# A two-mixer decoder step: a rebuilt opening, and the gate work of the first mixer moved between engines

## The reference

```python
h = _rmsnorm(x, norm_mix[i])
proj = h @ w_in                                   # (544, 4096): q, fz, i, g for 8 heads of 128
q = jax.nn.silu(q)
log_f = jnp.logaddexp(jnp.log(jnp.maximum(lb, LB_FLOOR)), jnp.log1p(-lb) + jax.nn.log_sigmoid(fz))
k = (1.0 - lb) * jax.nn.sigmoid(-fz)
o, S = _hgrn_recurrence(q, k, i, log_f, S0)       # S_t = diag(f_t) S_{t-1} + k_t v_t^T, o_t = S_t^T q_t
o = _rmsnorm(o, out_norm) * jax.nn.silu(g)
return o @ w_out, S
```

## Time and profile before

| | us |
|---|---|
| three runs, median (lowest, highest) | 1976.42 (1971.94, 1976.88) |
| the profiled execution's own time | 1976.46 |
| its span, first to last instruction | 1974.7 |
| PE busy in the span | 1811.3 |
| DVE busy | 1134.3 |
| ACT busy | 661.5 |

### The profile page before, as it was taken

One profiled execution on the slowest core, in us unless ns is written; L12 is line 12 of the kernel. 1 busy time (PEld: TensorE's weight loads), 2 busy tenths in 40 slices (PEclk: granted clock), 3 DMA queues, 4 the chain that ended last, 5 costly groups with the idle time before them and its releaser, 6 DMA issues. The chain is left out here.

```text
span 1974.7 us, 33936 instructions
## 1 busy us (share of the span) xinstructions
PE 1811.3 (92%) x13227; PEld 1714.2 (87%) x13227; DVE 1134.3 (57%) x2027; ACT 661.5 (33%) x1108; POOL 0.4 (0%) x5
## 2 busy tenths in 40 slices
PE   3899899998999999997799999999988999999997
PEld 3888888887999989997688888888867999999996
DVE  5777878785534334354666677667732643434344
ACT  1434444432212222222444455445522221222222
POOL 0000000000000000000000000000000000000000
PEclk9988989898999999998799999999957999999997
DMA  5122222222333323222112211211110333322321
GB/s 174 46 64 65 67 63 66 64 66 67 86 94 88 86 76 86 77 77 54 45 44 57 58 37 50 56 56 33 56 34 22 88 89 90 90 86 85 88 82 45
DMA packets 257436, 136.00 MB, mean 69 GB/s; under 512 B 6698, under 2 KB 255876, under 8 KB 257348
## 3 DMA queue, kind: packets, MB, share of 16 engines
q1 hardware_dynamic: 219700, 114.03, 20.4%
q10 hardware_dynamic: 37648, 20.68, 3.5%
HBM read 122.70 MB, written 12.00 MB: 68 GB/s over the span
## 5 line engine op out<-in xcount | busy, mean ns | idle before, releaser
L425 PE MATMUL pj<-xh,w_hi 128*128 128x272 f32 x2064 | 467.2, 309 | 29.8 <-DVE w_lo L1304 15.0
L425 PE MATMUL pj<-xl,w_hi 128*128 128x272 f32 x2064 | 440.4, 296 | 0.0
L425 PE MATMUL pj<-xh,w_lo 128*128 128x272 f32 x2064 | 439.4, 295 | 0.0
L865 ACT ACTIVATE w_hi<-w_raw 128x1024 fp32r<-128x1024 f32 x209 | 220.8, 1056 | 642.3 <-PE pj L425 623.9
L425 PEld LDWEIGHTS pj<-xh,w_hi 128*128 128x128 f32 x2064 | 335.6, 196 | 54.3 <-issue 26.8
L425 PEld LDWEIGHTS pj<-xl,w_hi 128*128 128x128 f32 x2064 | 338.5, 197 | 0.0
L425 PEld LDWEIGHTS pj<-xh,w_lo 128*128 128x128 f32 x2064 | 336.8, 197 | 0.0
L1304 DVE TENSOR_TENSOR w_lo<-w_raw,w_hi 128x1024 fp32r<-128x1024 f32 x209 | 254.8, 1219 | 45.9 <-ACT w_hi L865 45.7
L425 PE MATMUL pj<-oh,w_hi 128*128 128x272 f32 x1280 | 269.0, 292 | 12.7 <-DVE ol L1347 5.4
L425 PE MATMUL pj<-oh,w_lo 128*128 128x272 f32 x1280 | 266.0, 289 | 0.0
L425 PE MATMUL pj<-ol,w_hi 128*128 128x272 f32 x1280 | 266.0, 289 | 0.0
(11 more groups left out here) (275 smaller groups left out, 2050.8 us busy)
## 6 DMA issues: line engine op xcount, KB each, us to landing
w_raw<-in_mlp_w_up_dram SPq DMA_DIRECT2D x64, 512.0 KB, 3.9
w_raw<-in_mlp_w_down_dram SPq DMA_DIRECT2D x64, 512.0 KB, 3.7
w_raw<-in_hgrn_w_in_dram SPq DMA_DIRECT2D x32, 512.0 KB, 4.0
w_raw<-in_gdn_w_in_dram SPq DMA_DIRECT2D x32, 512.0 KB, 4.1
out_dram<-S ACTq DMA_DIRECT2D x16, 512.0 KB, 3.5
S<-in_state_hgrn_dram ACTq DMA_DIRECT2D x8, 512.0 KB, 4.0
w_raw<-in_hgrn_w_out_dram SPq DMA_DIRECT2D x8, 512.0 KB, 3.6
S<-in_state_gdn_dram ACTq DMA_DIRECT2D x8, 512.0 KB, 4.0
```

Of the source, the lines that this page charges most:

```text
L425: last = mm(pj[:, s, b, 0:HALF], w[:, s, k, :], v[:, k, b * HALF:(b + 1) * HALF], start=(k == 0 and a == 0), stop=(k == KT - 1 and a == 2))
L865: f(w_hi[:, c % SPLIT], w_raw[:, slot], ACT.Copy).then_inc(w_high, 1)
```

## The change

Five edits, in the program's order.

1. SP loads the identity, then all four blocks of `x` and the sample rows into five buffers without a wait, then the first four weight blocks, then the rest of `cf`, the masks (now bytes, no cast) and the two small arrays. The seven vector arrays are issued by ACT.
2. The turned blocks use PSUM banks 2, 3 and 0, 1 in turn; DVE copies blocks 0 and 2, ACT blocks 1 and 3. DVE's fills wait for nothing. The lower bounds come behind the eighth norm tile, with one more operation (`lb7`).
3. In the first norm ACT makes `xh` (a copy with a scale) and the square, DVE `xl` and the sum.
4. In a head's gate work the absolute values of fz, q, g and of the log-gate difference become ACT `Abs` instructions with the sign in the scale of the following `Exp`; K comes from ACT as one `Exp` with a bias; the factor of the log gate is folded into `Ln`, and `cd`, `cmax` and the add before the scan become one DVE operation.
5. In the tail of a head the scan, Q, level 1's differences, their exponential and its products (`d1`, `e1`, `kl1`) for the *next* head come ahead of `on`; eb and ebd come ahead of `rn`. At the head's start DVE does `d2`, `adiag`, kd, qe in that order.

```diff
@@ sync: the opening
-            sp.dma_start(cf[:], const_f).then_inc(c_in, c)
-            for stage_, part in zip(cstage, (const_u[:, 0:CU_HALF], const_u[:, CU_HALF:2 * CU_HALF])):
-                sp.dma_start(stage_, part).then_inc(c_in, c)
...
+            sp.dma_start(cf[:, 0:P], const_f[:, 0:P]).then_inc(eye_in, 16)
             for n in range(NC):
-                if n >= 2:
-                    sp.wait_ge(xs.sem, n - 1)
-                sp.dma_start(xrow[n % 2], x_prompt[0, n * P:(n + 1) * P, :]).then_inc(x_in[n % 2], 16)
+                sp.dma_start(xrow[n], x_prompt[0, n * P:(n + 1) * P, :]).then_inc(x_in[n], 16)
...
@@ scalar: the first norm
+                for i in (1, 3):
+                    sem_of(t, "t", i)
+                    s.did(f(xT[:, :, i * P:(i + 1) * P], rr[:, 0:2, :].rearrange("p a (k n) -> p (a k) n", n=P), ACT.Copy), "copy")
+                sem_of(s, "copy", 1)
+                high(0, 0)
...
+                for k in range(KT):
+                    s.did(f(xh[:, k], xT[:, k], ACT.Copy, scale=vec[:, V_MIX + k:V_MIX + k + 1]), f"hi{k}")
+                    if k >= 2:
+                        sem_of(v, f"acc{k - 2}", 0)
+                    s.did(f(sq[:, k % 2], xT[:, k], ACT.Square), f"sq{k}")
+                    if k == 1:
+                        high(0, 1)
+                lower_bounds()
@@ scalar: the gates
+                s.did(f(ng[:, row, 0:T], pr[:, row, 0:T], ACT.Abs), names[0])
+                s.did(f(ng[:, row, 0:T], ng[:, row, 0:T], ACT.Exp, scale=-1.0), names[1])
+                s.did(f(ng[:, row, 0:T], ng[:, row, 0:T], ACT.Ln, bias=1.0), names[2])
...
-                    sem_of(v, "nabs", h)
-                    s.did(f(pr[:, 1, 0:T], pr[:, 1, 0:T], ACT.Exp), "kexp")
-                    s.did(f(T1, T1, ACT.Exp), "cexp")
+                    sem_of(v, "fls", h)
+                    s.did(f(T1, ng[:, 1, 0:T], ACT.Abs, scale=-1.0, bias=hc[:, 3:4]), "nabs")
+                    s.did(f(T1, T1, ACT.Exp, scale=-1.0), "cexp")
+                    s.did(f(T1, T1, ACT.Ln, bias=hc[:, 0:1], scale=hc[:, 0:1]), "cln")
+                if slot == "K":
+                    sem_of(v, "fb", h)
+                    s.did(f(hg["K"], pr[:, 1, 0:T], ACT.Exp, bias=hc[:, 2:3]), "K")
@@ scalar: the tail of a head
+                    sem_of(v, "kl64", h)
+                    hgrn_prepare("K", nxt)
                     hgrn_prepare(7, nxt)
+                    hgrn_prepare("e1", nxt)
...
+                    hgrn_prepare(9, nxt)
                 sem_of(s, "ln", h)
                 s.did(f(sqr, sqr, ACT.Exp, scale=-0.5), "rn")
-                    hgrn_prepare(9, nxt)
@@ vector: the gates
-                    v.did(ts(T1, ng[:, 1, 0:T], hc[:, 2:3], hc[:, 1:2], ALU.add, ALU.subtract), "cd")
-                    v.did(stt(out=T1, in0=T1, scalar=-1.0, in1=T1, op0=ALU.mult, op1=ALU.min), "nabs")
-                    v.did(ts(ng[:, 1, 0:T], ng[:, 1, 0:T], hc[:, 2:3], hc[:, 1:2], ALU.add, ALU.max), "cmax")
-                    v.did(tt(ng[:, 1, 0:T], ng[:, 1, 0:T], T1, ALU.add), "lf")
+                    v.did(stt(out=ng[:, 1, 0:T], in0=ng[:, 1, 0:T], scalar=hc[:, 3:4], in1=T1, op0=ALU.max, op1=ALU.add), "lf")
+                if slot == "scan":
+                    v.did(nc.vector.tensor_tensor_scan(hg["b"], reset, ng[:, 1, 0:T], 0.0, ALU.mult, ALU.add), "scan")
+                    v.did(tt(hg["Q"], pr[:, 0, 0:T], ng[:, 0, 0:T], ALU.mult), "Q")
+                    v.did(apart_levels(0, 1), "d1")
+                    v.did(less_than_last(hg["bd"], hg["b"]), "bd")
                 if slot == 7:
                     v.did(log_sigmoid(2, T), "gls")
+                    after(s, "e1", h)
+                    v.did(scaled(0, 1), "kl1")
                     low(h * 4, U_HIN + 4)
-                if slot == 8:
...
@@ vector: a head's start
-                v.did(tt(qe, Q, eb, ALU.mult), "qe")
-                v.did(tt(kd, K, hg["bd"], ALU.mult), "kd")
-                differences(0, 1)
+                after(va, "kl1", h)
+                differences(1, 2)
                 after(t, "diag", h)
...
+                v.did(tt(kd, K, hg["bd"], ALU.mult), "kd")
+                v.did(tt(qe, Q, eb, ALU.mult), "qe")
                 low(h * 4, U_HIN + 5)
@@ vector: the tail of a head
                 if nxt is not None:
+                    hgrn_prepare("scan", nxt)
                     hgrn_prepare(7, nxt)
-                    hgrn_prepare(8, nxt)
                 out_tail(h, v, s, V_HON, hg["oo"], hg["sq"], hg["gate"], va)
```

More of the change, by code:

```diff
@@ L213, in build @@
         c_in = sem("constants_loaded")
-        x_in = [sem(f"x_loaded{n}") for n in range(2)]
+        eye_in = sem("identity_loaded")
+        vec_in = sem("vector_rows_loaded")
+        x_in = [sem(f"x_loaded{n}") for n in range(NC + 1)]
         st_in = sem("state_loaded")
@@ L225, in build @@
         VS = dict(
-            init=["masks", "fill", "vec", "cw", "lb1", "lb2", "lb3", "lb4", "lb5", "lb6"],
+            init=["fill", "vec", "cw", "lb1", "lb2", "lb3", "lb4", "lb5", "lb6", "lb7"],
             x=["copy"], xs=["copy"],
+            first=[f"{n}{k}" for k in range(KT) for n in ("lo", "acc")],
             norm=[f"{n}{k}" for k in range(KT) for n in ("acc", "hi", "lo")], normf=[f"acc{k}" for k in range(KT)],
-            ha=["cols", "fneg", "fls", "fb", "cd", "nabs", "cmax", "qneg", "qls", "lf", "gneg", "gls", "Q", "K", "scan",
-                "bd", "gate"],
-            hr=["qe", "kd", "d1", "adiag", "d2", "kl1", "d4", "kl2", "pred1", "d8", "kl4", "pred2", "d16", "kl8", "pred4",
+            ha=["cols", "fls", "fb", "qls", "lf", "scan", "Q", "d1", "bd", "gls", "kl1", "gate"],
+            hr=["d2", "adiag", "kd", "qe", "d4", "kl2", "pred1", "d8", "kl4", "pred2", "d16", "kl8", "pred4",
                 "d32", "kl16", "pred8", "S0", "S1", "S2", "S3", "d64", "kl32", "pred16", "vbig", "sdec", "kl64", "pred32",
@@ L262, in build @@
             init=["vec"], x=["t"], xs=["t"],
-            norm=["sum"], normf=["sum"],
+            first=["sum"], norm=["sum"], normf=["sum"],
             hr=["diag", "lv1", "lv2", "vT", "kdT", "lv4", "smp", "lv8", "dS", "lv16", "os", "lv32", "dSs", "lv64", "o", "ss"],
@@ L512, in level @@
                     more(tiles)
-                    pe.wait_ge(v.sem, v.after(f"kl{m}", h))
+                    if n == 0:
+                        pe.wait_ge(va.sem, va.after("kl1", h))
+                    else:
+                        pe.wait_ge(v.sem, v.after(f"kl{m}", h))
                     if n >= 2:
@@ L522, in level @@
                     t.did(last, f"lv{m}")
[L524 removed]
+                pe.wait_ge(va.sem, va.after("Q", h))
                 pe.wait_ge(st["ha"][1].sem, st["ha"][1].after("ebd", h))
@@ L1204, in _ @@
             load_state(state_hgrn, 0)
-            high(0, 0)
-            high(0, 1)
-            norm("n0", None)
-            for slot in range(3, 10):
+            first_norm()
+            for slot in (3, 4, 5, 6, "K", 7, "e1", 8, 9):
                 hgrn_prepare(slot, 0)
@@ L1807, in _ @@
             for k in range(KT):
-                norm_tile("n0", V_MIX, k)
+                first_norm_tile(k)
                 if k == 1:
                     low(0, 1)
+            lower_bounds()
+            dve.wait_ge(c_in, 16 * N_CONST)
             after(st["n0"][1], "rstd", 0)
-            for slot in range(2, 10):
+            for slot in (2, 3, 4, 5, 6, "scan", 7, 9):
                 hgrn_prepare(slot, 0)
```

254 lines of the change are left out of this document (132 added, 122 removed).

## The result

The changed kernel takes 1920.05 us (median of 4 runs, 1913.9 to 1921.96) against 1974.18 for the one before (4 runs, 1970.39 to 1976.88): a ratio of 0.9719, with a 95% interval of 0.9697 to 0.974. The forecast was 1929, in a range of 1915 to 1946. The profiled execution took 1921.42 us, its span is 1919.6, and its mean granted clock 0.94.

What follows compares the result with a forecast made beforehand. PE was taken to bound the kernel, fully in the MLP and not quite in the heads. From 1976.4 us, gains of 23.1 (opening), 2.0 (head 0), 21.6 (heads 1 to 6) and 1.0 (head 7) gave 1929, range 1915 to 1946.

Steps and rivals of the forecast that it cites:

- The bound: Whole kernel: PE bounds wherever weights are multiplied; in the heads it is busy 45.1 of 49.0 us, with clock 0.92.
- The opening: Start to `diag` of head 0: 17.7 gained to the first product, 1.1 to `rstd`, 4.3 to `diag`; 23.1 us together.
- a bound of 2.5 us: Opening: 2.5 us more is gained if the transposes of `x` run at the pace they have later.
- Head 0 and heads 1 to 6: Heads before the last: head 0 gains 2.0 us, heads 1 to 6 gain 3.6 each, 21.6 in all.
- what comes back at the head's start: Start of each head: unit 1's low part and `kl2` come late, so 1.0 of the 2.63 before level 1 returns.
- The 0.4 of ebd: Before `diag` of each head: eb and ebd ahead of `rn` end 0.57 earlier, so 0.4 us is gained.
- The clock: Heads: slow stretches behind waits cost 1.3 us each; 1.0 gained per head in 1 to 6, 1.4 in head 0.
- Head 7: Last head: PE waits for head 6's `lo`, 1.7 later, offsetting level 1's gain; 1.0 us is left without the slow stretch.
- The first: Rival, heads: waits come back with DVE further behind, slow stretches stay; 1.3 gained a head, 1944.5 us; chance 0.15.
- the third: Rival, opening: its transfers bind it and half of its gain goes, 11 us; 1940 us; chance 0.09.
- The second: Rival, heads: further slow stretches go, such as those at the sample products; 5.2 gained a head, 1917 us; chance 0.12.
- The fourth, table switches: Rival, ACT in heads: each `Abs` brings two table loads of 1.28 us, 10.2 a head; up to 2011 us; chance 0.03.

Runs made afterwards that it cites:

- `x_first`: The changed kernel with the vector arrays turned last, into the projections' banks, and the first hidden state loaded behind the first high part: 1913.37 us, ratio 0.9684.
- `rn_first`: The changed kernel with only eb and ebd put back behind `rn`: 1921.46 us, ratio 0.9719.
- `fill`: The kernel before the change, with eight extra matmuls in PE's wait before level 1 of each head, their result overwritten: 1957.87 us, ratio 0.9905.
- `pad`: The kernel before the change, with 16 products of ones with ones at the start of PE's list and nothing in the heads: 1958.51 us, ratio 0.9921.
- `v3`: `x_first` plus a later PE wait for head 6's `lo` in head 7 and 16 products of ones at PE's list start: 1898.61 us, ratio 0.9616.

## Why the prediction was right, step by step

**The bound** was read rightly: DVE's and ACT's busy time changed by 45.2 and 28.3 us, and only the places where PE waited or ran slowly turned into time. The rest of the program stood still to 0.7 us.

**The opening**, forecast -23.1, came to -21.96. The first product was forecast at 18.7 and came at 20.77. Two terms of it were off and partly cancelled. The vectors were to be there at "about 6" and came at 10.35: their seven loads, issued on ACT's queue from 0.75 to 3.6, move in packets of 512 B beside the 4096 B packets of `x` on SP's queue, and the forecast gave no row for its 6. Against that, the transposes took 1.46 a block (4.39 for three) and 1.06 for the last, not 1.92. Single transposes start 0.21 us apart until about 13.6, as in all blocks before, and 0.11 apart from then on. In `x_first`, where PE starts at 5.50, the change comes at about 9.0; before, with pauses between the blocks, it doesn't come. The granted clock reads 1.00 at both paces, so no row says what doubled the pace. The estimate had named that as a bound of 2.5 us. `x_first` shows what waiting for the vectors had cost, 5.0. From the first product on the count was good: `rstd` ended 13.5 later (forecast 14.5; a tile took 1.33 on DVE and not 1.42), `diag` 18.5 after that (forecast 18.4).

**Head 0 and heads 1 to 6**, forecast -23.6 together, came to -33.4. Idle time: forecast -16.2, measured -19.7. In heads 1 to 6 it fell by 3.1 per head, forecast 2.6. The waits that go were priced well: 2.63 before level 1, 0.55 for unit 2's low part (forecast 0.6), 0.35 before `diag` (forecast 0.4). The step that was mis-sized is what comes back at the head's start. 1.0 per head was to return as waits for low part 1 and level 2; 0.12 + 0.36 came back. DVE's `on` stood 1.1 before `diag` in the earlier trace rows; in after (timeline of DVE, `diag` at 231.56) it stands 0.3 behind it:

```profile
231.88 0.79 DVE L1387 SCALAR_TENSOR_TENSOR ws<-ws,vec 128x544 f32<-128x544 f32 x1 [2.64 <-ACT ws L1011]
```

So DVE starts the head 1.4 further back, where the forecast had 1.7, and that is most of the miss: low part 1 ends 8.69 behind `diag` (239.05 + 1.20; forecast 8.9) and `kl2` 10.07 (forecast 10.2), while PE reaches both places some 0.1 later than was counted. The 0.4 of ebd is real in the list of waits but isn't a gain of that edit, as `rn_first` shows; the waits at the head's start are its price.

**The clock** is the term that was mis-sized most: forecast -7.4 (6 x 1.0 and 1.4 in head 0), measured -13.7. The price of one slow stretch was about right, 1.3 forecast from the earlier trace rows: the two heads of after in the windows, with 323 and 322 matmuls and 0.79 of idle time each, are busy for 41.81 at clock 1.00 and 43.36 at 0.96, so 1.5 for one stretch of 3.4 us. It was the number that was wrong, and mostly in head 0. The trace of before has 17 such stretches in heads 0 to 6 (58.0 us), after has 8 (27.3). In heads 1 to 6 the forecast was nearly right: it let go the stretches behind level 1, five of them, and six went (one was double), while the seven others there stayed seven. At 1.5 each that is 9.0, where the forecast had taken 1.0 a head, 6.0. In head 0 it let go one, 1.4; three went, and PE's busy time fell by 4.8 (47.72 to 42.95). The two more were part of a stretch of 10.2 us that began 28 us behind `diag`, and after has one of the same length in head 1, at 27 us. What decides where these fall no trace shows, so more than half of this miss (3.4 of 6.3) has no shown cause. `fill` shows the mechanism for level 1 without the change: fill the wait, and the clock follows.

**Head 7** gave 0.42 of 1.0: the first output tile waited 2.46 for `lo` of head 6 where it had waited 0.85, because `lo` comes "1.7 later than before", as the forecast had it; the waits of 1.7 before level 1 and 0.4 before `diag` are gone from this head.

**The rivals.** The first (waits come back, 1944.5) and the third (transfers bind the opening, 1940) didn't occur, though the third's mechanism did at less than half of its price (5.0 of 11): it is what kept PE idle until 10.35. The second (the clock gives more, 1917) occurred in part, in head 0, which is why the result stands at 1920 and just below the forecast's own 1922 to 1937; its claim that the stretches at the sample products go in heads 1 to 6 did not hold. The misses didn't cancel: idle time and clock gave 3.5 and 6.3 more than forecast, and only 1.1 was missing in the opening and 0.6 in head 7. The fourth, table switches, is excluded by the trace: one load of 1.28 us in the whole program, and an `Abs` of 0.66 directly between an `Exp` and an `Exp`. By the Trainium skill (ScalarE: Activation LUTs, Table sets: the hidden batching unit), which puts abs into every set, that was to be expected; here the trace agrees.

## What to carry to other kernels

Where PE waits once in every iteration, ask what must have ended before the late operation can begin, and not how busy its engine is: 4.0 us less work per head on DVE moved the wait of 2.7 by nothing, and moving level 1 into the tail of the head before removed it. Price a wait on PE twice, once for itself and once for the slow clock that may follow it (1.5 us for every stretch of 3.4 us here), and don't expect all slow stretches to go with it. When two kernels' PE lists differ in length, compare them stretch by stretch before a gain is put down to an edit, since a shift of the list alone was worth 17 us here, 14.7 of them in one stretch. And read the releaser of a wait with care: a late low part was named for 2.8 us in which PE wasn't waiting for it.

## What was not expected of the hardware

- Small packets beside large ones (that this is the cause was not tried apart): seven arrays of together 73 KB, in 512 B packets on ACT's queue, landed up to 10.35, later than the first block of `x` (512 KB) on SP's queue, which PE could use from 5.50 in `x_first`.
- The stops of PE at the turn of its loop in the MLP, 2.8 and 2.0 us, twice in the first MLP, each followed by 6.8 us of slow clock; they go when the lengthened list moves the loop (14.7 us in all; `pad`, `v3` and `fill` are without them, the nine other kernels have them).
- An `Activation` with pointers for its scale and bias is longer than one with immediates: 0.64 to 0.66 without, 0.73 to 0.74 with one pointer, 0.84 with two, for the same 544 columns.
- The pace of the first transposes: 0.21 us apart until about 13.6 and 0.11 after that in the opening of after (the change comes at 9.0 in `x_first`), with the granted clock at 1.00 for both.
